# Two shift columns instead of four behind the tokens of an encoder step's projections

## The chip, the cores and the metric

The kernel runs on one core of a Trainium2 chip. The metric is the device time of one launch in microseconds, which covers both layers of the step. Engines are named as the profile names them: PE is TensorE's matmuls, PEld its weight loads, DVE is VectorE, ACT is ScalarE, POOL is GpSimd, SP the engine that issues the DMAs.

## The reference, cut to what matters

A stack of two layers works on 512 prompt tokens and 32 sample tokens with D = 1024 features. The prompt has one conditioning vector and the sample another, so each of the two groups has its own shift, scale and gate per feature. Each layer has three sub-layers: a SwiGLU feed-forward network, a mixer with attention and retention, and another feed-forward network.

```python
def rms_norm(x, g=None):
    xf = x.astype(jnp.float32)
    y = xf * lax.rsqrt(jnp.mean(jnp.square(xf), axis=-1, keepdims=True) + EPS)
...
def modulated_pre(x, g, mods, j):
    return rms_norm(x, g) * (1.0 + mods[:, 3 * j + 1, None]) + mods[:, 3 * j, None]

def swiglu(h, w1, w3, w2):
    return (jax.nn.silu(h @ w1) * (h @ w3)) @ w2
...
        h = modulated_pre(x, norm_pre[l, 0], mods, 0)
        x = gated_post(x, swiglu(h, ffn_w1[l, 0], ffn_w3[l, 0], ffn_w2[l, 0]), norm_post[l, 0], mods, 0, 0.5)
        h = modulated_pre(x, norm_pre[l, 1], mods, 1)
        o, st = mixer(h, l)
...
        z = h @ w_in[l]
```

What matters here is that the shift `mods[:, 3 * j]` is added to h in front of a projection, and that it is the same for all tokens of a group. A projection of h is therefore the projection of the scaled token, times its 1/rms, plus the projection of the shift. The kernel uses this: it projects the unnormalised tokens, and projects the shift vectors as further columns of the same matrix.

## The kernel before

Everything is stored with features on the 128 partitions and tokens along the row. The token matrix of a projection is `h`, with 8 row blocks of 128 features (index k). A row of h holds 544 tokens (prompt, then sample) and behind them the shift columns. Each float32 number is held as a sum of two float32r numbers, `h_hi` and `h_lo`, and so is each weight, `w_hi` and `w_lo`. A product is made of three float32r matmuls: hi times hi, lo times hi, and hi times lo.

A PSUM bank holds 512 columns of float32, so the tokens are cut in two halves. The first half has HT = 272 tokens. The second half has the other 272 tokens and the shift columns, HB columns in all. `tile3` (from L662) issues for each k six matmuls: with the weights `w_hi` the first half of `h_hi` and of `h_lo` (L669, L670), then the second half of both (L669, L670 again), and with `w_lo` the first and the second half of `h_hi` (L673). The same function, called without its last argument, makes the down projections, whose operand `u` has no shift columns: both halves have 272 columns there.

Three kinds of projections read h: the up projections of the two feed-forward networks of each layer (`up`, 22 features of 128 outputs, each with one chunk of weights for w1 and one for w3), and the input projection of the mixer (`z_tile`, 21 chunks). A chunk is 8 values of k times six matmuls, 48 in all. The first two chunks of each of the six sub-layers are issued by `first_high` and `first_tiles` in another order, since h becomes ready block by block then.

Weights come in chunks through two slots. SP loads a chunk into `raw`, ACT casts it to `w_hi` (`high`, `high_at`; L1176 or L1183) once PE has signalled by `w_used` that the slot is free, POOL subtracts to get `w_lo` (L546) and signals `lo_done`, for which PE waits at the start of a chunk. While PE multiplies from one slot, the other is filled.

When an up chunk is done, DVE multiplies the two halves by 1/rms from PSUM to SBUF (L1648, L1652) and copies the projected shift columns behind the tokens of `wide_s` or `wide_v` (L1649, L1653). ACT then applies Silu with the projected shift as its bias (L1300), DVE multiplies (L1657), ACT casts to `u_hi` (L1303) and DVE subtracts to get `u_lo` (L1662). In the mixer the same is done through `z_tmp` (L1695, L1696, then ACT at L1352 and L1353).

`wide_s`, `wide_v` and `z_tmp` have two rows of TW columns for each partition. Their tokens are used as scratch rows in many other places under the names `tmp_s` and `tmp_v`: the squares for the norms, the rotations in the mixer, and, seen as bf16, as the unused output of the dot products that compute the modulation vectors (`junk`, L1561), which DVE makes during the down projections.

The shift columns of h are written in the turn-over between two sub-layers: ACT writes those of `h_hi` (`shift_columns`, L1208) and DVE those of `h_lo` (`low_shift`, L1615), twice each, once for the prompt and once for the sample.

```python
T = NP_ + NS          # 544
HT = T // 2           # 272
TW = T + 4            # 548
HB = TW - HT          # 276
HP = T + 16           # length of a row of h_hi and h_lo in memory
```

Of the kernel before, what the change touches and what calls it, by code (L numbers as in the profile page):

```python
# [17 lines left out]
F32 = mybir.dt.float32  # L18
F32R = mybir.dt.float32r
BF16 = mybir.dt.bfloat16  # L20
ALU = mybir.AluOpType
# [3 lines left out]
P = 128  # L25
D = 1024
DEPTH = 2
NP_, NS = 512, 32
T = NP_ + NS
HT = T // 2  # L30
TW = T + 4
HB = TW - HT
HP = T + 16
PAST = 512
D_FF = 2816
KD = D // P
# [77 lines left out]
def streaming_trunk(nc, a, o):  # L114
    ctx = ExitStack()
    with ctx:
        def sb(name, shape, dt=F32):
            return ctx.enter_context(nc.sbuf_tensor(name, shape, dt))
# [22 lines left out]
        def signal(name, per_layer, before=0):  # L141
# [9 lines left out]

        wide_s = sb("wide_s", [P, 2, TW])
        wide_v = sb("wide_v", [P, 2, TW])
        tmp_s, tmp_v = wide_s[:, :, 0:T], wide_v[:, :, 0:T]
# [4 lines left out]
        mods = sb("mods", [P, 2, MODS])  # L159
# [42 lines left out]
        h_hi, h_lo, o_ffn, ada_w = hm["h_hi"], hm["h_lo"], hm["o_ffn"], hm["ada_w"]  # L202
# [7 lines left out]
             ("w_ukv", [P, 8, P], F32), ("state_in", [P, 4, VD], F32), ("state_p", [P, 4, VD], F32),  # L210
             [[("z_tmp", [P, 2, TW], F32)], [("k_n", [P, 4, 512], F32)]],
             [[("kpe_swap", [P, T], F32), ("q_pe_swap", [P, 2, T], F32), ("rope_tab", [P, 4, T], F32)],
# [19 lines left out]
        z_tmp, ada_first = um["z_tmp"], um["ada_first"]  # L232
# [50 lines left out]
        h_high = signal("h_high", 78)  # L283
        h_ready = signal("h_ready", 54)
# [4 lines left out]
        up_silu = signal("up_silu", 4 * FT)  # L289
# [94 lines left out]
        def x_count(j, t, m):  # L384

            return 2 * KD * j + KD * t + m + 1
# [781 lines left out]
        def _(act):  # L1168
# [35 lines left out]
            def shift_columns(l, j):  # L1204
                act.wait_ge(columns.sem, columns.at(l, COL_A if j else 0))
                for v in range(2):
                    c = 3 * j * KD
                    nc.scalar.copy(h_hi[:, :, T + 2 * v:T + 2 * v + 2],  # L1208
                                   mods[:, v, c:c + KD].unsqueeze(2).to_broadcast([P, KD, 2])).then_inc(h_high.sem, 1)

            def last_tile(l, j, chunk0, per_tile, o_buf, pre):

# [78 lines left out]
            def up(l, s):  # L1291
                base = FFN_C[s]

                def tile(i, f, last_width, ahead=True):
                    n = s * FT + i * 2 + f
                    for k in range(2) if ahead else ():
                        high_at(l, base, i * 2 + f + 1, k, last_width if f else KD * P)
                    act.wait_ge(up_out.sem, up_out.at(l, 2 * n + 1))
                    for v, at in enumerate((slice(0, NP_), slice(NP_, T))):
                        nc.scalar.activation(wide_s[:, f, at], wide_s[:, f, at], ACT.Silu,  # L1300
                                             bias=wide_s[:, f, T + 2 * v:T + 2 * v + 1]).then_inc(up_silu.sem, 1)
                    act.wait_ge(up_mul.sem, up_mul.at(l, 2 * n + 2))
                    nc.scalar.copy(u_hi[:, bass.ds(i * 2 + f, 1), :].rearrange("p a n -> p (a n)"),  # L1303
                                   tmp_v[:, f, :]).then_inc(up_hi.sem, 1)

                tile(0, 0, KD * P, ahead=False)
                tile(0, 1, KD * P)
                with act.Fori(1, FT // 2 - 1) as i:
                    tile(i, 0, KD * P)
                    tile(i, 1, KD * P)  # L1310
                tile(FT // 2 - 1, 0, KD * P)
                tile(FT // 2 - 1, 1, DN_T * P)
# [36 lines left out]
            def mixer(l):  # L1349
                def z_out(z, buf, dst, func=ACT.Identity):  # L1350
                    act.wait_ge(z_mul.sem, z_mul.at(l, z + 1))
                    nc.scalar.activation(dst[:, 0:NP_], z_tmp[:, buf, 0:NP_], func, bias=z_tmp[:, buf, T:T + 1])  # L1352
                    nc.scalar.activation(dst[:, NP_:T], z_tmp[:, buf, NP_:T], func, bias=z_tmp[:, buf, T + 2:T + 3])\  # L1353
                        .then_inc(z_ev.sem, 1)

                def square(n, buf, src):
# [161 lines left out]
        def _(dve):  # L1518
            v_ = nc.vector
# [60 lines left out]
            def turn_over(post, pre):  # L1580

                if post is not None:
                    l, j, o_buf = post
                    def invert(t):
                        dve.wait_ge(rooted.sem, rooted.at(l, 3 * j + 2 + t))
                        n = slice(t * TOK, (t + 1) * TOK)
                        v_.reciprocal(tok_inv[:, n], tok_root[:, n]).then_inc(inverted.sem, 1)  # L1587

                    for t in range(2):
                        n = slice(t * HT, (t + 1) * HT)  # L1590
                        invert(t)
                        dve.wait_ge(inv_spread.sem, inv_spread.at(l, 2 * j + t + 1))
                        for m in range(KD):
                            if t == 0 and m == KD - 1:
                                dve.wait_ge(half_ev.sem, half_ev.at(l, j + 1))
                            else:
                                dve.wait_ge(out_ev.sem, out_ev.at(l, j * KD + m + 1))
                            c = x_count(j, t, m)
                            prod = ps[:, 6 + m % 2, 0:HT]
                            if t or m >= 2:  # L1600

                                dve.wait_ge(x_new.sem, x_new.at(l, c - 2))
                            v_.tensor_tensor(prod, o_buf[:, m, n], ps[:, 4 + t, 0:HT], ALU.mult).then_inc(x_prod.sem, 1)
                            dve.wait_ge(x_prod.sem, x_prod.at(l, c))
                            v_.tensor_tensor(x[:, m, n], x[:, m, n], prod, ALU.add).then_inc(x_new.sem, 1)
                if pre is not None:
                    l, j = pre
                    first = not (l or j)

                    def low_shift():  # L1610
                        dve.wait_ge(columns.sem, columns.at(l, COL_A if j else 0))
                        dve.wait_ge(h_high.sem, h_high.at(l, 3 * KD + 2 if first else H_AT[j] + 2))
                        for v in range(2):
                            c = 3 * j * KD
                            v_.tensor_tensor(h_lo[:, :, T + 2 * v:T + 2 * v + 2],  # L1615
                                             mods[:, v, c:c + KD].unsqueeze(2).to_broadcast([P, KD, 2]),
                                             h_hi[:, :, T + 2 * v:T + 2 * v + 2].bitcast(F32),
                                             ALU.subtract).then_inc(h_ready.sem, 1)

                    if not first:  # L1620
                        low_shift()
                    for m in range(KD):
                        if first and m == 4:
                            dve.wait_ge(shift_mm.sem, 1)
                            for v in range(2):
                                v_.tensor_tensor(mods[:, v, 0:N_SHIFT], ps[:, 3, v:N_SHIFT * SHIFT_COLS:SHIFT_COLS],
                                                 ada_b[:, 0:N_SHIFT], ALU.add).then_inc(columns.sem, 1)
                        if first and m == LO_SHIFT:
                            low_shift()
                        if first and m % 2 == 0:  # L1630
                            dve.wait_ge(x_in[m // 2].sem, 16)
                        dve.wait_ge(h_high.sem, h_high.at(l, high_count(l, j, 1, m)))
                        for v, n in enumerate(GROUPS):
                            v_.scalar_tensor_tensor(out=h_lo[:, m, n], in0=x[:, m, n], scalar=mul_pre[:, j, v, m:m + 1],
                                                    in1=h_hi[:, m, n].bitcast(F32), op0=ALU.mult, op1=ALU.subtract)\
                                .then_inc(h_ready.sem, 1)
                    dve.wait_ge(rooted.sem, rooted.at(l, 3 * j + 1))
                    v_.reciprocal(rinv[:, :], root[:, :]).then_inc(inverted.sem, 1)

            def ffn(l, s):  # L1640
                with dve.Fori(0, FT // 2) as i:
                    for f in range(2):
# [12 lines left out]
                        dve.wait_ge(up_out.sem, up_out.at(l, 2 * n + 2))  # L1655
                        for v, at in enumerate(GROUPS):
                            v_.scalar_tensor_tensor(out=wide_v[:, f, at], in0=wide_v[:, f, at],  # L1657
                                                    scalar=wide_v[:, f, T + 2 * v:T + 2 * v + 1], in1=wide_s[:, f, at],
                                                    op0=ALU.add, op1=ALU.mult).then_inc(up_mul.sem, 1)
                        dve.wait_ge(up_hi.sem, up_hi.at(l, n + 1))  # L1660
                        at = bass.ds(i * 2 + f, 1)
# [407 lines left out]
```

## Time and profile before

| what | value |
|---|---|
| time, median of 3 runs | 2364.46 us (2363.18 to 2367.66) |
| span of the profiled execution, first to last instruction | 2360.0 us |
| PE busy | 2304.0 us, 98% of the span |
| PEld busy | 2184.5 us, 93% |
| DVE busy | 1220.4 us, 52% |
| POOL busy | 880.6 us, 37% |
| ACT busy | 821.1 us, 35% |
| mean granted TensorE clock | 0.981 of full speed |

The profiled execution is one of its own, and its span is the only time there is of it. The three timed runs lie 3.2 to 7.7 us above it, the median 4.5 us; the trace does not show what lies around the span. Busy shares of engines that work side by side don't add up.

### The profile page before, as it was taken

To read this page: it belongs to the slowest core of one execution; us is meant where nothing else is said; L and a number is where in the kernel's file an instruction comes from. 1 tells how busy PE (TensorE), PEld (TensorE's weight loads), DVE (VectorE), ACT (ScalarE), POOL (GpSimd) and SP (SyncE) were. 2 spreads that over 40 slices of the span, in tenths; PEclk is the share of its full clock that TensorE was granted. 3 is DMA by queue.
4 is the path that set the end of the run, shared out by engine and by line. 5 is a ranking of instruction groups with operands and counts; after the bars stand their busy time and mean duration, and the time that the engine had idled before them with its cause. 6 is when DMAs were issued, how large, how long until landed. Compare 5 with 4: busy or idle time off the path is not lost.

```text
span 2360.0 us, 43873 instructions
## 1 busy us (share of the span) xinstructions
PE 2304.0 (98%) x17694; PEld 2184.5 (93%) x17694; DVE 1220.4 (52%) x2065; ACT 821.1 (35%) x1392; POOL 880.6 (37%) x382
## 2 busy tenths in 40 slices
PE   8999999999999999999999999999999999999998
PEld 7999999899558899999999999999984699999998
DVE  5333379877561533338153333996846624333502
ACT  4323332433454433332243333225343553332321
POOL 2344334343113344344434334443321143433352
PEclk7999999999999999999999999999999999999999
DMA  6222268322211122236312223882231022222422
GB/s 233 90 83 86 89 238 312 136 86 81 73 37 54 60 84 89 89 113 246 123 58 86 89 89 110 296 289 75 82 111 51 1 72 73 88 89 89 163 86 75
DMA packets 70948, 263.82 MB, mean 112 GB/s; under 512 B 8704, under 2 KB 10112, under 8 KB 70336
## 3 DMA queue, kind: packets, MB, share of 16 engines
q1 hardware_dynamic: 70848, 262.44, 33.1%
q8 instruction: 69, 1.13, 0.2%
q14 instruction: 31, 0.25, 0.0%
HBM read 258.96 MB, written 3.45 MB: 111 GB/s over the span
## 4 chain that ended last, share of the span: by engine, by line
PE 75%; issue 10%; DVE 5%; POOL 4%; ACT 3%; DMA 1%; SPq 1%; POOLq 0%; DVEq 0%; ACTq 0%
PE ps L673 21%; PE ps L669 20%; PE ps L670 20%; POOL w_lo L546 4%; DVE wide_v L1561 2%; PE ps L679 1%; PE ps L745 1%; PE ps L1090 1%; PE ps L832 1%; PE ps L834 1%; PE ps L833 1%; PE ps L975 1%; DMA x<-in_x 1%; PE ps L1113 1%; PE ps L1057 1%
## 5 line engine op out<-in xcount | busy, mean ns | idle before, releaser
L546 POOL TENSOR_TENSOR w_lo<-raw,w_hi 128x1024 fp32r<-128x1024 f32 (+1 forms) x304 | 785.9, 2585 | 1296.2 <-ACT w_hi L1183 947.4
L669 PE MATMUL ps<-h_hi,w_hi 128*128 128x272 f32 x3296 | 886.8, 289 | 3.7 <-POOL w_lo L546 3.7
L670 PE MATMUL ps<-h_lo,w_hi 128*128 128x272 f32 x3296 | 889.4, 287 | 0.0
L673 PE MATMUL ps<-h_hi,w_lo 128*128 128x272 f32 x3296 | 685.7, 289 | 0.0
L669 PEld LDWEIGHTS ps<-h_hi,w_hi 128*128 128x128 f32 x3296 | 619.1, 188 | 5.2 <-POOL w_lo L546 5.0
L670 PEld LDWEIGHTS ps<-h_lo,w_hi 128*128 128x128 f32 x3296 | 620.9, 188 | 0.2
L1183 ACT CAST w_hi<-raw 128x1024 fp32r<-128x1024 f32 (+1 forms) x236 | 269.3, 1141 | 830.6 <-PE ps L673 809.0
L673 PEld LDWEIGHTS ps<-h_hi,w_lo 128*128 128x128 f32 x3296 | 519.2, 188 | 0.0
L669 PE MATMUL ps<-u_hi,w_hi 128*128 128x272 f32 x1232 | 332.7, 288 | 1.0 <-POOL w_lo L546 1.0
L670 PE MATMUL ps<-u_lo,w_hi 128*128 128x272 f32 x1232 | 332.4, 289 | 0.0
L1561 DVE CUSTOM_DVE_ANT_0 wide_v<-ada_w,ps,ada_b 128x1024 bf16<-128x1024 f32 x256 | 309.0, 1285 | 22.7 <-DMA ada_w<-in_ada 18.2
L1652 DVE TENSOR_TENSOR wide_v<-ps,rinv 128x544 f32<-128x544 f32 x88 | 63.8, 725 | 437.3 <-PE ps L673 437.3
L673 PE MATMUL ps<-u_hi,w_lo 128*128 128x272 f32 x1232 | 255.2, 288 | 0.0
L1657 DVE SCALAR_TENSOR_TENSOR wide_v<-wide_v,wide_s 128x512 f32<-128x512 f32 (+1 forms) x176 | 193.7, 1139 | 105.2 <-ACT wide_s L1300 105.2
L669 PEld LDWEIGHTS ps<-u_hi,w_hi 128*128 128x128 f32 x1232 | 231.7, 188 | 1.9 <-POOL w_lo L546 1.9
L670 PEld LDWEIGHTS ps<-u_lo,w_hi 128*128 128x128 f32 x1232 | 232.1, 188 | 0.0
L673 PEld LDWEIGHTS ps<-u_hi,w_lo 128*128 128x128 f32 x1232 | 192.8, 188 | 0.0
L1303 ACT CAST u_hi<-wide_v 128x544 f32 (+1 forms) x88 | 57.1, 649 | 213.6 <-DVE wide_v L1657 213.6
L1587 DVE RECIPROCAL tok_inv<-tok_root 128x3 f32<-128x3 f32 x12 | 2.1, 176 | 247.4 <-ACT tok_root L1191 247.4
L1176 ACT CAST w_hi<-raw 128x1024 fp32r<-128x1024 f32 x68 | 71.2, 1047 | 125.5 <-PE ps L673 82.5
L1662 DVE TENSOR_TENSOR u_lo<-wide_v,u_hi 128x544 f32 x88 | 63.8, 726 | 80.1 <-ACT u_hi L1303 80.1
L1300 ACT ACTIVATE wide_s<-wide_s 128x512 f32<-128x512 f32 (+1 forms) x176 | 82.2, 514 | 4.6 <-DVE wide_s L1649 4.6
(284 smaller groups left out, 2642.3 us busy)
## 6 DMA issues: line engine op xcount, KB each, us to landing
raw<-in_w_up SPq DMA_DIRECT2D x176, 512.0 KB, 3.5
ada_w<-in_ada SPq DMA_DIRECT2D x128, 512.0 KB, 5.2
raw<-in_w_dn SPq DMA_DIRECT2D x64, 704.0 KB, 4.8
raw<-in_w_mix SPq DMA_DIRECT2D x64, 512.0 KB, 3.6
ada_first<-in_ada SPq DMA_DIRECT2D x10, 512.0 KB, 7.8
decay<-in_decay SPq DMA_DIRECT2D x2, 2048.0 KB, 8.7
ada_first<-in_ada_first SPq DMA_DIRECT2D x6, 512.0 KB, 11.4
x<-in_x SPq DMA_DIRECT2D x4, 544.0 KB, 17.2
```

Source lines behind the costliest of these rows:

```text
L546: pool.tensor_tensor(w_lo[:, slot, 0:width], raw[:, slot, 0:width], w_hi[:, slot, 0:width].bitcast(F32), ALU.subtract).then_inc(lo_done.se ...
L669: pe.matmul(ps[:, bank + t, 0:width[t]], wh, hi[:, n], start=start, stop=False)
L670: pe.matmul(ps[:, bank + t, 0:width[t]], wh, lo[:, n], start=False, stop=False)
L673: last = pe.matmul(ps[:, bank + t, 0:width[t]], wl, hi[:, n], start=False, stop=stop)
L1176: nc.scalar.copy(w_hi[:, slot, 0:width], raw[:, slot, 0:width]).then_inc(hi_done.sem, 1)
L1183: nc.scalar.copy(w_hi[:, k, 0:width], raw[:, k, 0:width]).then_inc(hi_done.sem, 1)
L1300: nc.scalar.activation(wide_s[:, f, at], wide_s[:, f, at], ACT.Silu, bias=wide_s[:, f, T + 2 * v:T + 2 * v + 1]).then_inc(up_silu.sem, 1)
L1303: nc.scalar.copy(u_hi[:, bass.ds(i * 2 + f, 1), :].rearrange("p a n -> p (a n)"), tmp_v[:, f, :]).then_inc(up_hi.sem, 1)
L1561: v_.tensor_tensor_reduce(junk[v], ada_w[:, t, :], c_psum(v), 1.0, ada_b[:, b0 + t:b0 + t + 1], ALU.mult, ALU.add, mods[:, v, n0 + t:n0 + ...
L1652: v_.tensor_tensor(halves(tmp_v[:, f, :]), pair(4 * f + 2), halves(rinv[:, :]), ALU.mult)
L1657: v_.scalar_tensor_tensor(out=wide_v[:, f, at], in0=wide_v[:, f, at], scalar=wide_v[:, f, T + 2 * v:T + 2 * v + 1], in1=wide_s[:, f, at], ...
L1662: v_.tensor_tensor(u_lo[:, at, :].rearrange("p a n -> p (a n)"), tmp_v[:, f, :], u_hi[:, at, :].rearrange("p a n -> p (a n)").bitcast(F32) ...
```

## The change

Each shift vector stands in one column behind the tokens, where it stood in two equal ones. Four shift columns become two, so HB goes from 276 to 274 and TW from 548 to 546. The copies that write and move these columns are half as wide, and the places that read a projected shift as a bias or scalar find it one column, not two, further on for the sample. No instruction is added, removed or moved. The rows of h keep their length and place. The second row of `wide_s`, `wide_v` and `z_tmp` starts 2184 bytes behind the first, where it started 2192 bytes behind it; no tensor starts at another address.

```diff
@@ -28,7 +28,7 @@
 T = NP_ + NS
 HT = T // 2
-TW = T + 4
+TW = T + 2
 HB = TW - HT
...
@@ -1205,8 +1205,7 @@
                     c = 3 * j * KD
-                    nc.scalar.copy(h_hi[:, :, T + 2 * v:T + 2 * v + 2],
-                                   mods[:, v, c:c + KD].unsqueeze(2).to_broadcast([P, KD, 2])).then_inc(h_high.sem, 1)
+                    nc.scalar.copy(h_hi[:, :, T + v], mods[:, v, c:c + KD]).then_inc(h_high.sem, 1)
...
@@ -1298,7 +1297,7 @@
                         nc.scalar.activation(wide_s[:, f, at], wide_s[:, f, at], ACT.Silu,
-                                             bias=wide_s[:, f, T + 2 * v:T + 2 * v + 1]).then_inc(up_silu.sem, 1)
+                                             bias=wide_s[:, f, T + v:T + v + 1]).then_inc(up_silu.sem, 1)
...
@@ -1350,7 +1349,7 @@
-                    nc.scalar.activation(dst[:, NP_:T], z_tmp[:, buf, NP_:T], func, bias=z_tmp[:, buf, T + 2:T + 3])\
+                    nc.scalar.activation(dst[:, NP_:T], z_tmp[:, buf, NP_:T], func, bias=z_tmp[:, buf, T + 1:T + 2])\
                         .then_inc(z_ev.sem, 1)
...
@@ -1612,10 +1611,8 @@
-                            v_.tensor_tensor(h_lo[:, :, T + 2 * v:T + 2 * v + 2],
-                                             mods[:, v, c:c + KD].unsqueeze(2).to_broadcast([P, KD, 2]),
-                                             h_hi[:, :, T + 2 * v:T + 2 * v + 2].bitcast(F32),
-                                             ALU.subtract).then_inc(h_ready.sem, 1)
+                            v_.tensor_tensor(h_lo[:, :, T + v], mods[:, v, c:c + KD],
+                                             h_hi[:, :, T + v].bitcast(F32), ALU.subtract).then_inc(h_ready.sem, 1)
...
@@ -1655,7 +1652,7 @@
-                                                    scalar=wide_v[:, f, T + 2 * v:T + 2 * v + 1], in1=wide_s[:, f, at],
+                                                    scalar=wide_v[:, f, T + v:T + v + 1], in1=wide_s[:, f, at],
```

## Rows read from the trace of the kernel before

**Rows 1.** The page: span, PE's busy time, granted clock in 40 slices.

```profile
span 2360.0 us, 43873 instructions
...
PE 2304.0 (98%) x17694; PEld 2184.5 (93%) x17694; DVE 1220.4 (52%) x2065; ACT 821.1 (35%) x1392; POOL 880.6 (37%) x382
...
PEclk7999999999999999999999999999999999999999
```

**Rows 2.** PE's waits over the whole span: us in total, times, longest.

```profile
PE ps L735 <- ACT h_hi L1201: 10.0, 15, 1.4
PE ps L975 <- DVE ret_st L1791: 5.8, 6, 1.8
PE ps L669 <- POOL w_lo L546: 4.8, 8, 1.2
```

**Rows 3.** PE's groups by shape, with 276 columns: count | busy us, mean ns | idle before.

```profile
L669 PE MATMUL ps<-h_hi,w_hi 128*128 128x276 f32 x1648 | 477.7, 290 | 0.0
L670 PE MATMUL ps<-h_lo,w_hi 128*128 128x276 f32 x1648 | 475.6, 289 | 0.0
L673 PE MATMUL ps<-h_hi,w_lo 128*128 128x276 f32 x1648 | 475.2, 288 | 0.0
...
L745 PE MATMUL ps<-h_lo,w_hi 128*128 128x276 f32 x96 | 26.9, 302 | 0.0
...
L735 PE MATMUL ps<-h_hi,w_hi 128*128 128x276 f32 x80 | 24.1, 326 | 10.0 <-ACT h_hi L1201 10.0
...
L737 PE MATMUL ps<-h_hi,w_lo 128*128 128x276 f32 x80 | 22.5, 305 | 0.0
...
L657 PE MATMUL ps<-h_hi,w_hi 128*128 128x276 f32 x16 | 6.5, 412 | 2.9 <-ACT h_hi L1208 2.9
```

**Rows 4.** Timeline of DVE, first up projection: start us, us, what, [idle before].

```profile
80.50 0.72 DVE L1652 TENSOR_TENSOR wide_v<-ps,rinv 128x544 f32<-128x544 f32 x1 [5.25 <-PE ps L673]
...
310.02 0.72 DVE L1652 TENSOR_TENSOR wide_v<-ps,rinv 128x544 f32<-128x544 f32 x1 [5.25 <-PE ps L673]
```

**Rows 5.** Timeline of ACT, first down projection: its squares at a tile's end.

```profile
361.55 0.61 ACT L1326 ACTIVATE wide_s<-ps 128x544 f32<-128x544 f32 x1
...
427.84 0.62 ACT L1326 ACTIVATE wide_s<-ps 128x544 f32<-128x544 f32 x1
```

**Rows 6.** Timeline of PE at the end of the first down projection.

```profile
436.31 0.72 PE L686 MATMUL ps<-ones,squares 128*128 128x1 f32 x6
436.89 0.81 PE L686 MATMUL ps<-ones,wide_s 128*128 128x1 f32 x6
```

**Rows 7.** Timeline of all engines, up projection: a chunk's cast and subtraction, next cast.

```profile
201.30 1.05 ACT L1183 CAST w_hi<-raw 128x1024 fp32r<-128x1024 f32 x1 [4.91 <-PE ps L673]
...
202.43 2.39 POOL L546 TENSOR_TENSOR w_lo<-raw,w_hi 128x1024 fp32r<-128x1024 f32 x1 [3.56 <-ACT w_hi L1183]
...
207.42 1.06 ACT L1183 CAST w_hi<-raw 128x1024 fp32r<-128x1024 f32 x1 [1.12 <-PE ps L673]
```

**Rows 8.** Mixer: busy time from 522 to 574 us; PE's wait from 521 to 592.

```profile
core 0: us, PE busy (x) PEld busy (x) DVE busy (x) ACT busy (x) POOL busy (x), PEclk, DMA share, GB/s
522.00:574.00 52.00, 50.80 (x402) 50.37 (x400) 51.01 (x61) 15.32 (x24) 20.52 (x8) 1.00 0.27 81
...
PE ps L669 <- POOL w_lo L546: 1.9, 2, 1.2
```

**Rows 9.** The small copies of shift columns (by shape, DVE; by line, ACT and DVE).

```profile
L1649 DVE COPY wide_s<-ps 128x4 f32<-128x4 f32 x88 | 13.4, 152 | 0.0
...
L1208 ACT CAST h_hi<-mods x12: 195/204/208, 40.1 to 1931.0; 128x16 fp32r<-128x16 f32 x12
...
L1615 DVE TENSOR_TENSOR h_lo<-mods,h_hi x12: 163/177/759, 41.2 to 1944.9; 128x16 fp32r<-128x16 f32 x12
```

**Rows 10.** Timeline of DVE: the last dot product of the first down projection.

```profile
434.23 1.29 DVE L1561 CUSTOM_DVE_ANT_0 wide_v<-ada_w,ps,ada_b 128x1024 bf16<-128x1024 f32 x1
435.43 0.10 DVE L1561 DVE_READ_ACCUMULATOR2_ANT mods<- 128x1 f32 x1
```

## The prediction

> **What bounds the kernel now.** The page comes first: PE is busy for 2304.0 of 2360.0 us, and its granted clock is full (2.4 GHz) in all but the first of 40 slices [rows 1]. So the time is the number of matmuls times their spacing, and no other engine can give back more than the 56 us in which PE is idle. The list of PE's waits shows where part of that idle time lies: 10.0 us in the turn-overs, where the second halves of the first chunks wait for `h_hi`, 5.8 us in retention, which the change doesn't touch, and 4.8 us at chunk starts [rows 2]. Next come PE's groups by shape. The matmuls with 276 columns are 3 x 1648 in `tile3`, 96 + 80 + 80 in `first_tiles`, and 16 at L657 with 16 more at L659 of the same shape: 4944 + 256 + 32 = 5232 [rows 3]. Their mean of 288 to 290 ns is a latency and no price, since the next one starts long before they end.
>
> The price is the spacing, read from two steady stretches. In the first up projection DVE's L1652 starts when a feature is done on PE. From 80.50 to 310.02 us lie 19 features of 96 matmuls, half of them with 272 and half with 276 columns: 229.52 us / 1824 = 125.83 ns each [rows 4]. In the first down projection ACT's square starts when a tile is done. From 361.55 to 427.84 us lie 4 tiles of 132 matmuls, all with 272 columns: 66.29 us / 528 = 125.55 ns each [rows 5]. These stretches hold no wait of PE worth speaking of: in the up projection the weights of the next chunk are ready at 202.43 + 2.39 = 204.82 us and wanted some 2.5 us later, when the present chunk ends (ACT's next cast starts behind that end, at 207.42) [rows 7].
>
> So the average costs 0.28 ns more where half of the matmuls have four columns more. A matmul with 276 columns costs about 0.56 ns more than one with 272, which is 0.14 ns per column. At 2.4 GHz a column streamed in each cycle would be 0.417 ns. At this spacing a column is thus worth a third of a cycle's time, or there is a step between 272 and 276.
>
> **The change part by part.** It takes two columns from each of 5232 matmuls and adds nothing. First, how many of these are on the path that sets the end. In the mixer DVE is busy without a break from 522 to 574 us (51.01 of 52.00 us), and in and just after that stretch PE waits 1.9 us at chunk starts for weights whose chain goes through DVE (DVE scales a z tile, ACT writes it out and only then casts the next chunk) [rows 8]. Nine z tiles are computed there. What PE gains in them is waited away, since DVE's work is as long as before: 9 tiles x 24 matmuls x 2 layers = 432. The 160 at L735 and L737 have a wait of 10.0 us for `h_hi` among them [rows 3], so I leave them out too. That leaves 5232 - 432 - 160 = 4640.
>
> Second, the price of two columns. Nothing in the trace has 274 columns. The bounds:
> - From below, 0: the spacing of 125 ns holds something that has nothing to do with columns. Six matmul records with a single column start within 436.89 - 436.31 = 0.58 us, 97 ns each [rows 6]. Nearly four fifths of the spacing is there with one column.
> - From above, one cycle of 2.4 GHz per column: 0.83 ns for two, 4640 x 0.83 = 3.9 us.
> - Between them, 0.28 ns if the measured difference of 0.56 is spread evenly over four columns, 4640 x 0.28 = 1.3 us; and 0.56 ns if 125.55 ns is a floor that 274 columns reach, 2.6 us.
>
> I take 0.28 ns, the even spread, as it is nearest to the rows: they are the same three matmuls on the same engine and differ in the width alone.
>
> A rule is to be weighed here. The Trainium skill, "TensorE: Matmul & The Clock Gate", section "Back-to-back issue gap", gives columns / 2.4 + 2.5 ns for a matmul by itself, which is 115.8 ns for 272 columns, and by it two columns would be 0.83 ns and the sum 3.9 us. The trace disagrees with its level: 125.55 ns. The same section gives 81 ns at 128 and 131 ns at 512 columns for streams in which each matmul has its own weight load, which is what this kernel issues; that is 0.13 ns per column, close to the 0.14 above, and an estimate from it is 4640 x 0.26 = 1.2 us.
>
> Third, the small operations. DVE's copies of the projected shift (152 ns for 4 elements) become 2 elements wide, the shift columns of `h_hi` (204 ns for 16) and `h_lo` (177 ns, mostly) become 8 [rows 9]. As 4 and 16 elements cost so nearly the same, hardly any of it is per element. The copies of the projected shift lie under PE, DVE waiting 5.25 us for it at the next chunk [rows 4]. The others come 24 times in all. At 204 ns they are 4.9 us; were a tenth of that to go, it would be 0.5 us, in a turn-over where PE waits for ACT. I cost it at nothing and keep 0.5 us for the range.
>
> Fourth, the second rows of `wide_s`, `wide_v` and `z_tmp` start 8 bytes earlier, which is 8 bytes off a multiple of 16 where they were on one. Nothing large in the trace starts like that, so its price has no row; I take 0 (the same operations on these rows run in the same time on the first and the second row now) and treat a loss as a rival.
>
> **The sum.** 4640 x 0.28 ns = 1.3 us less: the span goes from 2360.0 to 2358.7. The median of the three runs stands 4.5 us above the span, and I move it by the same amount: 2364.46 - 1.3 = 2363.2 us, 0.05% less. The three runs themselves spread over 4.5 us. About 0.2%, 4.7 us, is what a measurement of this kernel can tell from no change.
>
> **The rivals.**
>
> *A whole cycle per column.* The extra 12 ns of the spacing is then a fixed gap between matmuls, and columns stream at one per cycle. For it speaks that the up stretch comes to 302.0 cycles per matmul at 2.4 GHz, exactly 28 more than its mean of 274 columns; against it that the down stretch comes to 301.3, and 272 + 28 would be 300. It gives 2364.5 - 3.9 = 2360.6. The floor, which 274 columns reach, gives 2361.9.
>
> *No change at all.* The measured 0.56 ns may be a step for a last, part-filled group of columns behind the 272, and a group of two may cost what a group of four does. Nothing in the rows speaks against it, since they hold two widths only. It gives 2364.5. The Trainium skill, "SBUF — State Buffer", section "Specifications (TRN2)", says that memory is read in lines of 16 bytes, which are four such columns; by that rule 274 columns touch as many lines as 276. No run here has shown it.
>
> *Slower: the second rows.* During the down projections DVE makes dot products whose unused output goes to the rows of `wide_v` in turn. In the first down projection of a layer there are 96, half of them writing the second row, and they follow each other without a gap. The last ends at 435.43 + 0.10 = 435.53 us [rows 10], and PE needs them all before its sums of squares at 436.31 [rows 6]. So there is 0.78 us of slack, and the rival decides from 0.78 / 48 = 16 ns per dot product on. If the output at the new start cost a tenth more (0.13 us of 1.29), 48 of them would be 6.2 us, 5.4 us of it on the path, twice: 2364.5 + 10.9 - 1.3 = 2374. For it speaks only that nothing like it is in the trace; against it that the first and second rows behave alike now.
>
> **How the numbers follow.** The even spread has 0.42, a whole cycle per column 0.20, the floor 0.12, no change 0.18, slower by the second rows 0.08. The predicted time is that of the even spread, 2363.2. Only the last case is slower by more than 0.2%: 0.08. None of the others reaches 0.2% by itself (2359.7 us): the dearest column gives 2360.6. With the spread of the runs and 0.5 us for the small copies I give faster 0.11, a third of the whole-cycle case and some of the floor. The rest, 0.81, is within 0.2%. The range goes from below the whole-cycle case, 2359.8, to 2366.3, no change with the scatter of the runs on it; it leaves out the second rows and a part of the scatter.
>
> **What would show it.** The distance between DVE's L1652 rows in the up projection: 12.08 us per feature now; 12.07 by the even spread (125.69 ns), 12.05 by the floor (125.55), 12.04 by a whole cycle per column (125.42), 12.08 by no change. The down projection's tiles should stay at 16.57 us. The wait of 1.9 us in the mixer should grow by some tenths. The dot products of L1561 should stay at 1.28 us on both rows, and PE should ask for them at the same distance after the last one. The prediction would be wrong if 274 columns cost more than 276, because two is a worse remainder than four: 0.5 ns more for each would be 2.6 us. It would also be wrong if another engine's operations on the shifted rows became longer and PE's waits in the turn-overs or the mixer grew by microseconds.

## The result and the profile after

The changed kernel takes 2368.69 us (median of 9 runs, 2367.68 to 2373.38), the kernel before 2363.18 us beside it (9 runs, 2360.3 to 2367.66). The ratio is 1.0026 [1.0017, 1.0036]: slower by a quarter of a per cent, and above the range of the prediction.

The page of the changed kernel has first the span and the busy times, then the granted clock in 40 slices. They answer to [rows 1].

```profile
span 2365.9 us, 43873 instructions
PE 2310.7 (98%) x17694; PEld 2191.9 (93%) x17694; DVE 1218.7 (52%) x2065; ACT 819.0 (35%) x1392; POOL 872.5 (37%) x382
PEclk8999999999999999999999999999999999999999
```

The span grew by 5.9 us and PE's busy time by 6.7 us, at the same number of instructions and the same full clock (2.4 GHz from the second slice on). The other engines have less to do than before. So PE did not wait more; its matmuls took longer. The list of PE's waits says the same, against [rows 2]:

```profile
PE ps L735 <- ACT h_hi L1201: 8.4, 15, 1.2
PE ps L975 <- DVE ret_st L1788: 5.8, 6, 1.8
PE ps L669 <- POOL w_lo L546: 4.7, 8, 1.2
```

The wait for `h_hi` in the turn-overs became shorter by 1.6 us, and the two others stayed. So did the wait for `w_lo` in the mixer, in PE's waits from 521 to 594 us, against [rows 8]:

```profile
PE ps L669 <- POOL w_lo L546: 1.9, 2, 1.2
```

The rows that price the matmuls are DVE's, one per feature of an up projection. These are the first and the last that the 19 features of each of the four up projections lie between, in the changed kernel (L1649, start in us first; it was L1652 before):

```profile
80.08 0.72 DVE L1649 TENSOR_TENSOR wide_v<-ps,rinv 128x544 f32<-128x544 f32 x1 [5.30 <-PE ps L673]
311.63 0.73 DVE L1649 TENSOR_TENSOR wide_v<-ps,rinv 128x544 f32<-128x544 f32 x1 [5.30 <-PE ps L673]
825.99 0.72 DVE L1649 TENSOR_TENSOR wide_v<-ps,rinv 128x544 f32<-128x544 f32 x1 [5.30 <-PE ps L673]
1057.54 0.73 DVE L1649 TENSOR_TENSOR wide_v<-ps,rinv 128x544 f32<-128x544 f32 x1 [5.30 <-PE ps L673]
1241.05 0.72 DVE L1649 TENSOR_TENSOR wide_v<-ps,rinv 128x544 f32<-128x544 f32 x1 [5.25 <-PE ps L673]
1472.60 0.72 DVE L1649 TENSOR_TENSOR wide_v<-ps,rinv 128x544 f32<-128x544 f32 x1 [5.30 <-PE ps L673]
1986.81 0.72 DVE L1649 TENSOR_TENSOR wide_v<-ps,rinv 128x544 f32<-128x544 f32 x1 [5.30 <-PE ps L673]
2218.35 0.72 DVE L1649 TENSOR_TENSOR wide_v<-ps,rinv 128x544 f32<-128x544 f32 x1 [5.30 <-PE ps L673]
```

And in the kernel before, for the second to the fourth up projection (the first stands in [rows 4]):

```profile
825.84 0.72 DVE L1652 TENSOR_TENSOR wide_v<-ps,rinv 128x544 f32<-128x544 f32 x1 [5.25 <-PE ps L673]
1055.36 0.72 DVE L1652 TENSOR_TENSOR wide_v<-ps,rinv 128x544 f32<-128x544 f32 x1 [5.25 <-PE ps L673]
1239.20 0.72 DVE L1652 TENSOR_TENSOR wide_v<-ps,rinv 128x544 f32<-128x544 f32 x1 [5.14 <-PE ps L673]
1468.72 0.72 DVE L1652 TENSOR_TENSOR wide_v<-ps,rinv 128x544 f32<-128x544 f32 x1 [5.25 <-PE ps L673]
1982.82 0.72 DVE L1652 TENSOR_TENSOR wide_v<-ps,rinv 128x544 f32<-128x544 f32 x1 [5.25 <-PE ps L673]
2212.34 0.72 DVE L1652 TENSOR_TENSOR wide_v<-ps,rinv 128x544 f32<-128x544 f32 x1 [5.25 <-PE ps L673]
```

Each pair spans 229.52 us before and 231.55 after. So 19 features take 2.03 us longer, every time the same, and four times that is 8.1 us, more than the whole loss. Per feature it is 12.19 us instead of 12.08, per matmul 126.95 ns instead of 125.83. Half of these matmuls are unchanged at 272 columns. Set down to the other half, the loss is 2.2 ns **more** for each matmul with 274 columns than for one with 276. That is a price per changed matmul, and not what one such matmul takes by itself. By the start times of PE's records in these four stretches, a group of six matmuls loses 6.7 ns in the mean, and 3.9 ns of it lie between the starts of its first and its second matmul (124.25 ns before, 128.17 after), which both have 272 columns.

Follow the distance between the two kernels along the run. The changed one is 0.42 us ahead at the first row, 1.61 behind at the second. Then it is 0.15, 2.18, 1.85, 3.88, 3.99 and 6.01 behind, and 5.9 at the end of the span. It loses 2.03 in each up projection and gains back 1.46 and 0.33 after the first and the second of them. After the third it loses 0.11. So a loss of 8.1 us stands against a balance of 2.2 us gained elsewhere. Further matmuls with 274 columns lie there too: the 21 z tiles of the first mixer take 117.55 us from the first to the last and not 116.94. The 1.46 can't be put down to the change, for attention differs by as much within the kernel before: from DVE's last z tile to ACT's first square of the output projection (590.54 to 730.73 us) it takes 140.2 us in its first layer and 138.7 in its second, and the changed kernel takes 138.7 in both.

The down projection did not move. ACT's squares, between which 4 tiles lie, against [rows 5]:

```profile
363.12 0.61 ACT L1325 ACTIVATE wide_s<-ps 128x544 f32<-128x544 f32 x1
429.42 0.61 ACT L1325 ACTIVATE wide_s<-ps 128x544 f32<-128x544 f32 x1
```

That is 66.30 us for 528 matmuls, 66.29 before. The slower rival's place, the end of the first down projection's dot products on DVE, against [rows 10]:

```profile
435.04 1.27 DVE L1560 CUSTOM_DVE_ANT_0 wide_v<-ada_w,ps,ada_b 128x1024 bf16<-128x1024 f32 x1
436.24 0.08 DVE L1560 DVE_READ_ACCUMULATOR2_ANT mods<- 128x1 f32 x1
```

A dot product takes 1.27 us and not more than the 1.29 before. The chain ends at 436.32. PE's sums of squares, in the same kernel's order of time, against [rows 6]:

```profile
437.87 0.72 PE L686 MATMUL ps<-ones,squares 128*128 128x1 f32 x6
```

They start 1.55 us after the last dot product, so nothing waits there.

### The profile page after: what moved, and what is told of

It is laid out like the page before. It is cut to its first block, busy times and chain, and to the rows that moved or that the text cites. A ratio compares the mean times of both kernels' runs of the same rounds, so it can differ in the third digit from the quotient of the medians.

```text
span 2365.9 us, 43873 instructions
## 1 busy us (share of the span) xinstructions
PE 2310.7 (98%) x17694; PEld 2191.9 (93%) x17694; DVE 1218.7 (52%) x2065; ACT 819.0 (35%) x1392; POOL 872.5 (37%) x382
## 4 chain that ended last, share of the span: by engine, by line
PE 75%; issue 11%; DVE 6%; POOL 4%; ACT 3%; DMA 1%; SPq 1%; POOLq 0%; DVEq 0%; ACTq 0%
PE ps L673 21%; PE ps L669 21%; PE ps L670 20%; POOL w_lo L546 4%; DVE wide_v L1560 2%; PE ps L679 1%; PE ps L745 1%; PE ps L1090 1%; PE ps L832 1%; PE ps L834 1%; PE ps L833 1%; PE ps L975 1%; DMA x<-in_x 1%; DVE ps L1602 1%; PE ps L1057 1%
## 5 line engine op out<-in xcount | busy, mean ns | idle before, releaser
L1560 DVE CUSTOM_DVE_ANT_0 wide_v<-ada_w,ps,ada_b 128x1024 bf16<-128x1024 f32 x256 | 309.1, 1275 | 21.0 <-DMA ada_w<-in_ada 16.4
L1649 DVE TENSOR_TENSOR wide_v<-ps,rinv 128x544 f32<-128x544 f32 x88 | 63.7, 724 | 442.0 <-PE ps L673 442.0
```

The source lines that it names most:

```text
L1560: v_.tensor_tensor_reduce(junk[v], ada_w[:, t, :], c_psum(v), 1.0, ada_b[:, b0 + t:b0 + t + 1], ALU.mult, ALU.add, mods[:, v, n0 + t:n0 + ...
L1649: v_.tensor_tensor(halves(tmp_v[:, f, :]), pair(4 * f + 2), halves(rinv[:, :]), ALU.mult)
```

## The experiments

All kernels are the kernel before with a few lines changed. R is the number of copies of each shift column in `h` (2 before, 1 in the change), so the second halves have 272 + 2R columns. TW is the length of a row of `wide_s`, `wide_v` and `z_tmp` (548 before, 546 in the change). HP is the length of a row of `h` (560 in both, 2240 bytes). From `w274_hp552` on, TW is 546 in all kernels but `w276_rows547`. Lines up to the middle of the program are one higher than before. Two projected columns are copied out in each of these kernels, at T and T+1. The expectations call theories by letters, as they came up:

- A: a matmul of 274 columns is dearer than one of 276. Within it, A1: because two is a worse remainder than four. A2, later P: because of where the columns lie, width and place together. W: 274 is dearer everywhere.
- B: the loss comes from the shorter rows of `wide_s` and its like, or from the copies.
- Q: a gain comes from POOL's sums of squares, whose inputs now start elsewhere.

### The two parts apart

`w276_rows546` keeps 276 columns and takes the short rows:

```diff
-TW = T + 4
-HB = TW - HT
+R = 2
+TW = 546
+HB = HT + 2 * R
...
-            return ps[:, b + 1, HT:HB]
+            return ps[:, b + 1, HT:HB:R]
...
-                                             bias=wide_s[:, f, T + 2 * v:T + 2 * v + 1]).then_inc(up_silu.sem, 1)
+                                             bias=wide_s[:, f, T + v:T + v + 1]).then_inc(up_silu.sem, 1)
...
-                        v_.tensor_copy(wide_v[:, f, T:TW], biases(4 * f + 2)).then_inc(up_out.sem, 1)
+                        v_.tensor_copy(wide_v[:, f, T:T + 2], biases(4 * f + 2)).then_inc(up_out.sem, 1)
```

> Matmuls hold 276 columns again, every shift column twice, but only two projected columns are copied out and the rows of wide_s, wide_v and z_tmp keep the changed length of 546. Theory A (the width of 274 columns itself costs): a feature of the up projection takes 12.08 us as before the change (125.83 ns per matmul) and the time is that of the kernel before, within 0.1%. Theory B (the shifted second rows or the copies cost): the time stays 0.2 to 0.3% above the kernel before, and a feature takes 12.19 us.

`w274_rows548` is the opposite: `R = 1` and `TW = 548`, which is the change with the rows left long.

> Matmuls hold 274 columns as after the change, but the rows of wide_s, wide_v and z_tmp have their old length of 548, so that no second row starts off a multiple of 16 bytes. Theory A (width): a feature takes 12.19 us (126.94 ns per matmul), and the time is 0.2 to 0.3% above the kernel before. Theory B (rows or copies): 12.08 us and the time of the kernel before.

Measured: short rows alone 0.9985 [0.9976, 0.9994] (2359.51 us against 2362.16), 274 columns alone 1.0049 [1.0035, 1.0062] (2373.92). The same two DVE rows of the first up projection, for `w276_rows546`:

```profile
80.03 0.72 DVE L1653 TENSOR_TENSOR wide_v<-ps,rinv 128x544 f32<-128x544 f32 x1 [5.25 <-PE ps L674]
309.55 0.73 DVE L1653 TENSOR_TENSOR wide_v<-ps,rinv 128x544 f32<-128x544 f32 x1 [5.25 <-PE ps L674]
```

and for `w274_rows548`:

```profile
80.61 0.72 DVE L1653 TENSOR_TENSOR wide_v<-ps,rinv 128x544 f32<-128x544 f32 x1 [5.30 <-PE ps L674]
312.16 0.72 DVE L1653 TENSOR_TENSOR wide_v<-ps,rinv 128x544 f32<-128x544 f32 x1 [5.30 <-PE ps L674]
```

229.52 and 231.55 us: the spacing goes with the columns, and the rows have no part in it. B falls and A holds. The 11.8 us that 274 columns cost by themselves are 5232 times 2.2 ns, the price from the stretch. The interval, 8.3 to 14.6 us, doesn't tell whether all 5232 pay or only the 4640 that the prediction counted. The shorter rows are a gain of 2.7 us, and the two parts together (1.0049 x 0.9985 = 1.0034) agree with the 1.0026 [1.0017, 1.0036] of the change.

### A remainder of two, or a slope?

`w280` (`R = 4`) and `w278` (`R = 3`), both with `TW = 548`:

> Every shift column four times: second halves of 280 columns, a whole number of groups of four behind 272. Theory A1 (a remainder of two behind a multiple of four costs, the rest goes by columns): 0.56 ns for each further four columns, so 126.1 ns per matmul and 12.11 us per feature, 0.1 to 0.15% above the kernel before. Theory A2 (the cost comes from how the reads of a width fall against each other and against the weight loads, and is not ordered by width): any spacing from 125.5 to 128 ns; below 125.83 or above 126.5 ns would speak for it.

> Every shift column three times: second halves of 278 columns, again a remainder of two. Theory A1 (remainder): what 274 has over a line through 272, 276 and 280 comes back, some 1.25 ns on the average of a matmul, so about 127.2 ns and 12.21 us per feature. Theory A2 (not ordered by width): another spacing, below 126.3 ns for example.

`w280` took 1.0018 [1.0009, 1.0027], `w278` 2366.46 us in its one run. The rows of `w278`, whose width leaves a remainder of two over four as 274 does:

```profile
80.33 0.72 DVE L1653 TENSOR_TENSOR wide_v<-ps,rinv 128x544 f32<-128x544 f32 x1 [5.26 <-PE ps L674]
310.36 0.72 DVE L1653 TENSOR_TENSOR wide_v<-ps,rinv 128x544 f32<-128x544 f32 x1 [5.26 <-PE ps L674]
```

and of `w280`:

```profile
80.46 0.72 DVE L1653 TENSOR_TENSOR wide_v<-ps,rinv 128x544 f32<-128x544 f32 x1 [5.28 <-PE ps L674]
311.00 0.72 DVE L1653 TENSOR_TENSOR wide_v<-ps,rinv 128x544 f32<-128x544 f32 x1 [5.28 <-PE ps L674]
```

The spacing is 126.11 ns at 278 and 126.39 at 280. From 276 (125.83) each two columns add 0.28 ns to the mean. 278 lies on that line, so A1 falls. For 280, A1 had 126.1 and A2 looked below 125.83 or above 126.5; 126.39 is neither. 274 alone lies off the line by more than 1 ns.

### Another place for the same columns

`HP` sets the distance between two row blocks of h, and with it where `h_lo` and all that lies behind it begin: with 8 elements less per row `h_lo` starts 256 bytes earlier and the operand of the down projection 512. `w274_hp552` and `w276_hp552` have the rows shorter by 8 elements (`HP = T + 8`, with `R = 1` and `R = 2`, both with `TW = 546`):

```diff
-HP = T + 16
+HP = T + 8
```

> Matmuls of 274 columns as after the change, but the rows of h_hi and h_lo lie 2208 bytes apart and not 2240. Theory W (274 columns cost by their number alone, wherever the rows lie): 126.9 ns per matmul, 12.19 us per feature, 0.2 to 0.3% above the kernel before. Theory P (places: the extra comes from how reads of this length fall against the places of the rows, so it goes with the distance of the rows): a spacing at least 0.4 ns away from 126.94, most likely below 126.2 ns and then within 0.1% of the kernel before.

> Matmuls of 276 columns with rows of h 2208 bytes apart, not 2240. Theory W: 125.83 ns as before the change, 12.08 us per feature. Theory P: another spacing, by 0.2 ns or more to either side.

`w274_base32` leaves the distance and moves `h_hi` and all behind it by 32 bytes:

```diff
-        sb("h_front", [P, 48])
+        sb("h_front", [P, 56])
```

> As after the change, rows of h 2240 bytes apart, but h_hi, h_lo and all that lies behind them start 32 bytes later. Theory W: 126.94 ns. Theory P says which start counts: if only the distances of the rows count, 126.94 ns as well; if the start against some line of the memory counts, another spacing, and then the down projection, whose operand moves too, may leave 125.55 ns.

Measured: 0.9995 [0.9985, 1.0006] and 1.0008 [0.9998, 1.0018], and 2365.35 us in the one run of `w274_base32`. The rows of `w274_hp552`:

```profile
80.02 0.72 DVE L1653 TENSOR_TENSOR wide_v<-ps,rinv 128x544 f32<-128x544 f32 x1 [5.27 <-PE ps L674]
310.30 0.72 DVE L1653 TENSOR_TENSOR wide_v<-ps,rinv 128x544 f32<-128x544 f32 x1 [5.27 <-PE ps L674]
```

The spacing falls to 126.25 ns with 8 elements of padding gone that nothing reads. For 276 columns at the same place, in `w276_hp552`, it rises to 126.39:

```profile
80.34 0.72 DVE L1653 TENSOR_TENSOR wide_v<-ps,rinv 128x544 f32<-128x544 f32 x1 [5.29 <-PE ps L674]
310.87 0.73 DVE L1653 TENSOR_TENSOR wide_v<-ps,rinv 128x544 f32<-128x544 f32 x1 [5.29 <-PE ps L674]
```

So the place of the rows is part of the price, at either width, and here 274 is the cheaper one.

### No shift columns at all

`w272` has `R = 0`. It leaves out the projections of the shift; values of two tokens stand in as biases.

> No shift columns in the matmuls at all: both halves 272 columns (the projections of the shift are left out, and values of two tokens stand in their place as biases). Rows of h 2240 bytes apart. Theory W: 125.55 ns as in the down projection, whose matmuls are as wide, so 12.05 us per feature. Theory P: it may be another number than 125.55, since the rows of the down projection's operand lie 2176 bytes apart; the line through 276, 278 and 280 columns (125.83, 126.10, 126.40) would give 125.27 ns.

```profile
80.07 0.72 DVE L1653 TENSOR_TENSOR wide_v<-ps,rinv 128x544 f32<-128x544 f32 x1 [5.21 <-PE ps L674]
308.07 0.72 DVE L1653 TENSOR_TENSOR wide_v<-ps,rinv 128x544 f32<-128x544 f32 x1 [5.21 <-PE ps L674]
```

Those are the rows of `w272`: 228.00 us or 125.00 ns, which is 300.0 cycles of 2.4 GHz, 28 more than the columns. Neither 125.55 nor 125.27 had it. The kernel took 2351.56 us in its one run. With 276 columns the stretch holds 302.0 cycles for 274 columns in the mean, again 28 more [rows 4]. At this place 272 and 276 columns thus stand exactly one cycle per column apart, and 274 (304.7 cycles for a mean of 273 columns) is not between them.

### How far does the place go, and what did the short rows bring?

Two more row lengths for 274 columns, `HP = T + 4` and `HP = T + 12`:

> Matmuls of 274 columns, rows of h 2192 bytes apart (2240 after the change, 2208 in w274_hp552). Theory P (places): a third spacing, beside 126.94 and 126.25 ns; without any loss by places it would be (273 + 28) cycles of 2.4 GHz, 125.42 ns, since 272 and 276 columns at 2240 bytes have shown columns + 28 cycles (125.00 and 125.83 ns). Theory W (274 columns always cost more than 276): above 125.83 ns wherever the rows lie.

> The same with rows of h 2224 bytes apart. Theory P: again another spacing between 125.42 and 127 ns. Theory W: above 125.83 ns. If 2192, 2208, 2224 and 2240 all stay above 125.83 ns, theory W is left as a tendency, though not as a fixed price.

276 columns moved by 32 bytes (`R = 2`, `h_front` 56):

> Matmuls of 276 columns, rows of wide_s 546 long, and h_hi and all behind it 32 bytes later. 274 columns went from 126.94 to 126.67 ns by this shift. Theory P: the spacing of 276 columns leaves 125.83 ns too. If it stays at 125.83, the start counts only for 274 columns.

And `w276_rows546` with one element more per row (`TW = 547`), a length at which the second rows start 12 bytes off a multiple of 16 from the first and not 8:

> Matmuls of 276 columns, rows of wide_s, wide_v and z_tmp 547 long, so that the second row starts 12 bytes past a multiple of 16 (8 bytes past it at 546, 0 at 548). Theory Q (POOL's sums of squares run slower when both of their inputs start at the same place within 16 bytes, and the turn-overs wait for them): its first sum takes 1.15 us as with 546 and not 1.35 us, and the time is 0.1 to 0.2% below the kernel before, as with 546. Theory N (the gain with rows of 546 is scatter): the time of the kernel before within 0.05%, whatever the sums take.

`w274_hp548` took 1.0046 [1.003, 1.0063] and `w274_hp556` 0.9991 [0.9981, 1.0001]. Rows of the first:

```profile
80.10 0.72 DVE L1653 TENSOR_TENSOR wide_v<-ps,rinv 128x544 f32<-128x544 f32 x1 [5.31 <-PE ps L674]
311.90 0.73 DVE L1653 TENSOR_TENSOR wide_v<-ps,rinv 128x544 f32<-128x544 f32 x1 [5.31 <-PE ps L674]
```

and of the second:

```profile
80.22 0.73 DVE L1653 TENSOR_TENSOR wide_v<-ps,rinv 128x544 f32<-128x544 f32 x1 [5.25 <-PE ps L674]
310.00 0.72 DVE L1653 TENSOR_TENSOR wide_v<-ps,rinv 128x544 f32<-128x544 f32 x1 [5.26 <-PE ps L674]
```

127.08 and 125.98 ns: with 274 columns, 32 bytes of row length, with the moves that follow from them, are worth 1.1 ns on each of the up projections' matmuls. `w276_base32` shows that such a shift also moves matmuls whose width nobody touched. Its down projection, of 272 columns:

```profile
361.68 0.61 ACT L1327 ACTIVATE wide_s<-ps 128x544 f32<-128x544 f32 x1
427.82 0.62 ACT L1327 ACTIVATE wide_s<-ps 128x544 f32<-128x544 f32 x1
```

This is 66.14 us for 528 matmuls, 125.27 ns, against 125.55 before [rows 5]. All spacings, read in the same two rows of the first up projection (ns per matmul, a mean over as many with 272 columns as with the width given):

| bytes from row block to row block of h | 272 | 274 | 276 | 278 | 280 |
|---|---|---|---|---|---|
| 2192 | | 127.08 | | | |
| 2208 | | 126.25 | 126.39 | | |
| 2224 | | 125.98 | | | |
| 2240 (both kernels) | 125.00 | 126.95 | 125.83 | 126.11 | 126.39 |
| 2240, all 32 bytes on | | 126.67 | 126.11 | | |

So W's fixed surcharge falls, since at 2208 bytes 274 columns are cheaper than 276. That the price changes with width and place (A2, P) holds. No place tried gives 274 columns less than the 125.83 of the kernel before.

Width and place are still not all. The second and the fourth down projection of `w276_rows546` are the same matmuls on the same rows. ACT's squares, again 4 tiles apart:

```profile
1106.32 0.61 ACT L1327 ACTIVATE wide_s<-ps 128x544 f32<-128x544 f32 x1
1172.90 0.62 ACT L1327 ACTIVATE wide_s<-ps 128x544 f32<-128x544 f32 x1
2263.03 0.62 ACT L1327 ACTIVATE wide_s<-ps 128x544 f32<-128x544 f32 x1
2329.33 0.61 ACT L1327 ACTIVATE wide_s<-ps 128x544 f32<-128x544 f32 x1
```

That is 66.58 us (126.10 ns per matmul) in the second and 66.30 (125.57) in the fourth, or 1816 and 1808 cycles of 2.4 GHz for six matmuls. The kernel before has the shorter spacing in all four of its down projections, and `w280`, whose operand lies at the same place, the longer one in all four. The up projections show one spacing in all four of each trace, and the same one again in the kernels that share width and place (three with 276 columns, two with 274). What picks the spacing, in reading the rows, loading the weights or the way a stretch begins, stays open.

Q is read in POOL's groups by shape (count, then busy us and mean ns, then idle time before it) and in ACT's squares, which wait for them. The kernel before:

```profile
L557 POOL TENSOR_TENSOR squares<-wide_s 128x544 f32<-128x544 f32 x6 | 8.1, 1357 | 0.0
L566 POOL TENSOR_TENSOR squares<-squares,wide_s 128x544 f32<-128x544 f32 x12 | 17.7, 1476 | 5.5 <-ACT wide_s L1263 4.6
L1263 ACT ACTIVATE wide_s<-x 128x544 f32<-128x544 f32 x48 | 31.0, 653 | 25.1 <-PE ps L679 12.4 <-POOL squares L566 6.5 <-POOL squares L563 6.2
```

The changed kernel:

```profile
L557 POOL TENSOR_TENSOR squares<-wide_s 128x544 f32<-128x544 f32 x6 | 6.9, 1146 | 0.0
L566 POOL TENSOR_TENSOR squares<-squares,wide_s 128x544 f32<-128x544 f32 x12 | 16.5, 1372 | 5.5 <-ACT wide_s L1262 4.6
L1262 ACT ACTIVATE wide_s<-x 128x544 f32<-128x544 f32 x48 | 31.1, 651 | 22.7 <-PE ps L679 12.4 <-POOL squares L566 5.3 <-POOL squares L563 4.9
```

`w276_rows546`:

```profile
L558 POOL TENSOR_TENSOR squares<-wide_s 128x544 f32<-128x544 f32 x6 | 6.9, 1151 | 0.0
L1264 ACT ACTIVATE wide_s<-x 128x544 f32<-128x544 f32 x48 | 31.1, 651 | 23.2 <-PE ps L680 12.9 <-POOL squares L567 5.3 <-POOL squares L564 5.0
```

And `w276_rows547`:

```profile
L558 POOL TENSOR_TENSOR squares<-wide_s 128x544 f32<-128x544 f32 x6 | 8.2, 1372 | 0.0
L1264 ACT ACTIVATE wide_s<-x 128x544 f32<-128x544 f32 x48 | 30.9, 650 | 25.1 <-PE ps L680 12.2 <-POOL squares L567 6.6 <-POOL squares L564 6.2
```

ACT waits 12.7 us for the sums before, 10.2 after, 10.3 with the short rows alone and 12.8 with rows of 547. I had expected rows of 547 to have the fast sums too; they don't. But the time went the way of the sums: 1.0005 [0.9996, 1.0015] with rows of 547, no gain, at the same spacing of 125.83 ns and with the same narrow copies. So the copies are not the gain, and the 2.5 us less of waiting are about the 2.7 us of `w276_rows546`. In the traces the difference lies in the turn-overs. Add up the time from the start to the second feature, and from ACT's last square in each of the next five down or output projections to the first z tile or the second feature that follows: it is 309.3 us before, 307.2 with rows of 546 and 309.1 with 547. The last five of the six take 238.0 to 239.7 us in the nine kernels with rows of 546, and 240.8 to 242.0 in the five others. The spans of the three traces (2360.0, 2359.1 and 2358.7 us) don't show it, since attention and the down projections differ from trace to trace by as much. DVE's 48 small operations on `h_lo` follow the same division (333 ns with rows of 546, 354 to 356 with 547 and 548). They may own a part of the gain; no run separates them from the sums.

`w276_rows546` has the lowest ratio of the kernels that do all the work and were run more than once. Its interval lies below that of the changed kernel and below the kernel before. From `w274_hp556`, which keeps the 274 columns, it is not told apart.

## Why the prediction was wrong

- **What bounds the kernel.** Right: the loss is in PE's spacing, and the other engines only give back what shortens PE's turn-overs.
- **The price of two columns: this step failed.** The prediction chose 0.28 ns less per matmul, "as it is nearest to the rows: they are the same three matmuls on the same engine and differ in the width alone". They don't differ in the width alone. The 272 columns of the down projection are read from rows 2176 bytes apart, the 276 from rows 2240 bytes apart. With both at 2240 bytes the difference is 0.83 ns in the mean, three times the 0.28 that was read. So the two points between which the even spread was drawn were not of one kind. How much of the difference is the place's is not shown, since the down projection itself knows two spacings: at 126.10 ns, where other traces have it, its 272 columns would have stood above the 276. That it stood at 125.55 in the one trace that was read was luck. Two points at the same place would not have saved it either, as the whole slope gives 0.83 ns less for two columns, 3.9 us faster. What failed is that a third width was read off the line through two.
- **Its bounds.** They ran from 0 to 0.83 ns of gain. The measured value is a loss of 2.2 ns for each changed matmul (126.95 against 125.83 in the mean), on the side for which no bound was given. Two widths can't exclude it: nothing showed that the price grows steadily from one to the other.
- **The sentence on what would make it wrong** named the event, 274 columns dearer than 276. The cause that it gave, that two is a worse remainder than four, fell with `w278`, and its size, 0.5 ns, was a quarter of the true one.
- **A whole cycle per column.** Its arithmetic holds between 272 and 276 columns at 2240 bytes, but its forecast for 274 (125.42 ns) was 1.5 ns off.
- **No change at all, and the floor.** Both fell with the spacing. The Trainium skill, "SBUF — State Buffer", section "Specifications (TRN2)", says that memory is read in lines of 16 bytes, by which 274 columns touch as many lines as 276. The trace doesn't agree with a price by lines: 126.95 against 125.83 ns.
- **The second rows, "I take 0".** Wrong in the other direction: they are the gain of 2.7 us, most likely by the 0.2 us less for each of POOL's first sums, which no run shows apart from DVE's operations on `h_lo`. The prediction looked for a loss on DVE's dot products, which stayed at their time, and didn't ask which operations read two rows at once and are waited for.
- **The down projection at 16.57 us per tile, the wait for `w_lo` in the mixer, the small copies at nothing.** The first is right (66.30 / 4 = 16.57). The wait was to grow by tenths and stayed at 1.9 us, as PE gained nothing to wait with. That 9 of 21 z tiles were left out fits in total: a layer's z tiles became 0.6 us longer, where 2.2 ns on all of their changed matmuls would be 1.1. The copies are at nothing as far as rows of 547 tell.

The sum as it should have stood: 5232 x 2.23 = 11.7 us more for the matmuls, or 10.3 for 4640 of them, 2.7 less for the shorter rows. That is 7.6 to 9.0 us. The span shows 5.9 and the medians 5.5. In the two traces 1.5 us of the rest is attention's first layer; for the medians the rest lies within the intervals of the two parts.

## What to carry to other kernels

Fewer columns are not cheaper by themselves: where matmuls follow each other at 125 ns, the place of the rows that they read moved the price by as much as several columns did, so compare widths only at equal places, read more than one stretch of the same matmuls, and try a padding or two before judging a width. When an edit changes the length of a row, look through the trace for every operation that reads two rows at once, and ask who waits for it. Take an edit with two effects apart before it is dropped: here its unnoticed half was the better kernel.

## What was not expected of the hardware

- The spacing of float32r matmuls, with a weight load for each, doesn't grow steadily with the columns: 125.00, 126.95, 125.83, 126.11 and 126.39 ns for 272 to 280 in steps of two, at one place. For 274 columns it ran from 125.98 to 127.08 with the place alone. For 272 columns of the down projection, 32 bytes moved it from 125.55 to 125.27.
- The same matmuls on the same rows can run at either of two steady spacings: 125.57 and 126.10 ns in two down projections of one trace.
- POOL's addition of two rows of 544 float32 takes 1.36 us when the second row starts 2192 bytes behind the first, 1.37 us at 2188 bytes and 1.15 us at 2184. No other distances were tried, so that it goes by the remainder over 16 (0, 12 and 8) is not shown.
